# Relative bias loaded in two parts behind a branch chunk, attention outputs behind dense tiles, squares gathered on VectorE

## Chip, cores and metric

The kernel runs on one core of a Trainium2 chip. The metric is the device time in microseconds of one execution. One number is the median of several runs; the profile is of one further execution, with its own time.

## What is computed

Two layers of a decoder trunk on 512 tokens of width 1024, all in float32. Cut to what matters here:

```
x += 1/2 * gate1 * postnorm(SwiGLU(mod(prenorm(x))))     # feed-forward 1, width 2816
x +=       gate2 * postnorm(HybridMixer(mod(prenorm(x))))
x += 1/2 * gate3 * postnorm(SwiGLU(mod(prenorm(x))))     # feed-forward 2
# HybridMixer: one projection into GLA / differential attention / S5 / branch gates,
# each branch projected (w_branch[0..2]), merged by sigmoid gates, then w_out
logits = q @ k.T + bias[t5_bucket(dist)]                 # 8 maps, 4 heads of two maps
a = softmax(map 0) - lam * softmax(map 1);  o = a @ v;  o *= rsqrt(mean(o*o))
y *= rsqrt(mean(y*y, axis=-1) + 1e-6) * norm_post        # the post-norm of each sub-layer
```

## The kernel before

Activations lie transposed (channel on the partition, 512 tokens along the free axis). The weights come as chunks of 1 MB. SyncE loads each chunk into one of two places `raw[0]`, `raw[1]`; ScalarE copies it to a high part (`split`, L1278) and VectorE subtracts to get the low part (L1745). Each dense product is three matmuls, high by high, high by low and low by high (`matmul3`, L633 to L635); a tile of 128 outputs by 512 tokens with 8 input blocks is 24 matmuls, one with 4 input blocks is 12. A load waits until the split of the chunk two places earlier is done, a split waits until TensorE is done with that chunk. Every engine runs its own list in order, written out by hand; semaphores tie them.

**The mixer.** The list `MIXER` orders the chunks. Around the change they are `glu1, glu0, bs0, bs1, dq0, dq1, dk0 ... dv1, gg0, gg1, bg0, gg2, gg3, bg1, gd0 ...`, then `wo0..wo3` (the output projection). `ys` is the split of the S5 branch output, which `bs0` multiplies; the GLA decays (`gla_alpha` on TensorE, L1624 to L1636 on ScalarE, L2397 to L2412 on VectorE) run beside `dq0` and `dq1`. After the GLA heads (`o_ready` counts them) the GLA output `gr` is split into `yga_hi` (ScalarE, L1535) and `yga_lo` (VectorE, L2240), and `bg0` multiplies it. ScalarE and VectorE each split `bg0`: ScalarE before its `yga` splits, VectorE after them.

**The bias.** `bias_tab` (8 maps, 128 by 512 each, 2 MB) takes the place of `gq`, `gk`, `gv`, so SyncE waits for `o_ready` of all four GLA heads, then issues eight DMAs of 16 partitions (L613), and only then the load of `bg0`. VectorE waits for all eight before `diff_max` of step 0.

**The attention loop** has 16 steps i, head hd = i // 4, query block qb = i % 4. In step i TensorE does `diff_scores(i + 1)` (L1082), at the first step of a new head `diff_out` of the head before (L1098), one dense tile of `BESIDE_DIFF[i]`, at that same step `head_ms` (L1045, sums of squares of the head's output), and `diff_turn(i)` (transposes, L1091). VectorE does `diff_max(i + 1)` (bias and row maximum, L2285), at a new head `head_keep` (L2244, waits for `head_ms`), then `diff_mix(i)` (L2297 to L2300 and L1738), on which `diff_turn(i)` waits. ScalarE does the exponentials (L1555), `head_squares` at a new head (L1540, L1543), the sigmoids of gate tiles (L1461) and `diff_copy(i)` (L1565).

**A boundary** follows each of the six sub-layers (q = 0..5; 1 and 4 are the mixers', 5 the last). As each of the 8 output tiles ends, ScalarE copies it scaled to `y_sub` (L1321) and squares it to `sq_buf` (L1324); VectorE multiplies `y_sub` by `h` and adds up the products (L1793, L1798); TensorE adds the squares over channels with one block of 8 small matmuls per tile (`y_square_sums`, L647: column 0 plain, column 1 weighted by `sum_w`), each issued one tile late. After the last tile `norms` issues the blocks of tiles 6 and 7, the cross sums (`cross_total`, `cross_last`, L654), and then the root (L1342), its spread over rows (L675) and the normalization follow, before the next sub-layer can start.

## Time and profile before

| | |
|---|---|
| median of 3 runs | 2732.19 us (2730.94 to 2732.38) |
| the profiled execution | 2733.83 us, its span 2731.9 us |
| TensorE busy with matmuls | 2654.0 us, 97% |
| VectorE busy | 1396.2 us, 51% |
| ScalarE busy | 963.1 us, 35% |
| DMA engines | 35.2% of 16, mean 112 GB/s |
| mean granted TensorE clock | 0.979 of full |

All stretches below are in microseconds from the start of the span. The start of one instruction to the start of the next on TensorE is what it costs there; the printed length also holds the pipeline and is longer.

### The profile page before, as it was taken

Reading aid. Unit: us, or ns where it says so; the run is one execution under the profiler, and the core shown is the slowest. Engines: PE = TensorE matmul, PEld = TensorE weight load, DVE = VectorE, ACT = ScalarE, POOL = GpSimd, SP = SyncE. Lnnn points to the kernel's source line nnn. Section 1 sums busy time; section 2 is a strip of 40 time slices with the busy share of each in tenths; the row PEclk is TensorE's granted clock in tenths of the full one; section 3 lists DMA queues with packets and bytes.
Section 4 is the critical chain, followed back from the end, with each engine's and each line's share of the span. In section 5 each row is a group of like instructions: output and inputs, shape, how many; then the busy total and the mean of one; then the engine's idle time right before and its main releaser. Section 6 shows DMA issues by size and latency. Waiting matters only on the chain.

```text
span 2731.9 us, 34428 instructions
## 1 busy us (share of the span) xinstructions
PE 2654.0 (97%) x12925; PEld 2210.4 (81%) x12925; DVE 1396.2 (51%) x2146; ACT 963.1 (35%) x1177; POOL 75.1 (3%) x64
## 2 busy tenths in 40 slices
PE   6999999999989999999999999999999899999998
PEld 5888888987866888888888888899878578888886
DVE  5777326755245558532277752386342545653322
ACT  3333224644245432222142221346332643322212
POOL 0000001200000000000000000031000000000000
PEclk7999999999999999999999999999999999999999
DMA  8675222222241236322247633222223212332321
GB/s 260 200 229 178 100 92 74 78 70 93 62 93 61 79 108 213 126 92 100 100 139 231 225 113 104 74 82 78 87 86 62 83 62 93 108 123 95 105 92 47
DMA packets 268426, 306.99 MB, mean 112 GB/s; under 512 B 17783, under 2 KB 245499, under 8 KB 268324
## 3 DMA queue, kind: packets, MB, share of 16 engines
q1 hardware_dynamic: 268172, 305.23, 35.2%
q8 instruction: 71, 1.16, 0.2%
q10 hardware_dynamic: 152, 0.35, 0.0%
q14 instruction: 31, 0.25, 0.0%
HBM read 303.44 MB, written 2.45 MB: 112 GB/s over the span
## 4 chain that ended last, share of the span: by engine, by line
PE 91%; DVE 3%; ACT 2%; DMA 2%; issue 1%; SPq 1%; ACTq 0%; DVEq 0%
PE bank L633 26%; PE bank L635 25%; PE bank L634 25%; DMA raw<-in_w_branch 1%; PE bank L898 1%; PE bank L647 1%; PE bank L899 1%; PE bank L900 1%; PE bank L765 1%; PE bank L1098 1%; PE bank L1215 1%; PE bank L1062 1%; PE bank L1082 1%; PE bank L964 1%; PE bank L980 1%
## 5 line engine op out<-in xcount | busy, mean ns | idle before, releaser
L1745 DVE TENSOR_TENSOR w_both_lo<-raw,w_both_hi 128x2048 fp32r<-128x2048 f32 x200 | 459.6, 2298 | 619.5 <-ACT w_both_hi L1278 618.8
L633 PE MATMUL bank<-u_hi,w_both_hi 128*128 128x512 f32 x1928 | 763.0, 396 | 5.3 <-DVE u_lo L1738 2.6
L635 PE MATMUL bank<-u_hi,w_both_lo 128*128 128x512 f32 x1928 | 753.1, 391 | 0.0
L634 PE MATMUL bank<-u_lo,w_both_hi 128*128 128x512 f32 x1928 | 752.3, 390 | 0.0
L1278 ACT ACTIVATE w_both_hi<-raw 128x2048 fp32r<-128x2048 f32 x200 | 380.4, 1902 | 731.4 <-PE bank L635 702.3
L633 PEld LDWEIGHTS bank<-u_hi,w_both_hi 128*128 128x128 f32 x1928 | 363.4, 188 | 89.0 <-issue 7.5
L635 PEld LDWEIGHTS bank<-u_hi,w_both_lo 128*128 128x128 f32 x1928 | 362.9, 188 | 77.7
L634 PEld LDWEIGHTS bank<-u_lo,w_both_hi 128*128 128x128 f32 x1928 | 363.5, 189 | 73.0
L633 PE MATMUL bank<-g_hi,w_both_hi 128*128 (+1 forms) x704 | 276.2, 392 | 0.0
L635 PE MATMUL bank<-g_hi,w_both_lo 128*128 (+1 forms) x704 | 274.0, 389 | 0.0
L634 PE MATMUL bank<-g_lo,w_both_hi 128*128 (+1 forms) x704 | 274.0, 389 | 0.0
L1738 DVE SCALAR_TENSOR_TENSOR ada_acc<-ada_w,cond,ada_acc 128x256 f32<-128x256 f32 x448 | 217.2, 485 | 16.0
L1376 ACT ACTIVATE g_hi<-silu_buf 128x512 f32 (+1 forms) x88 | 55.6, 632 | 317.5 <-DVE silu_buf L1871 317.4
L635 PEld LDWEIGHTS bank<-g_hi,w_both_lo 128*128 128x128 f32 x704 | 132.1, 188 | 27.7
L634 PEld LDWEIGHTS bank<-g_lo,w_both_hi 128*128 128x128 f32 x704 | 132.3, 188 | 26.7
L633 PEld LDWEIGHTS bank<-g_hi,w_both_hi 128*128 128x128 f32 x704 | 132.2, 188 | 26.5
L1871 DVE TENSOR_TENSOR silu_buf<-silu_buf,bank 128x512 f32<-128x512 f32 x88 | 60.2, 686 | 182.4 <-PE bank L635 182.4
L898 PE MATMUL bank<-w_both_hi,u_hi 128*128 128x256 f32 x256 | 75.9, 297 | 0.0
L900 PE MATMUL bank<-w_both_lo,u_hi 128*128 128x256 f32 x256 | 72.5, 283 | 0.0
L899 PE MATMUL bank<-w_both_hi,u_lo 128*128 128x256 f32 x256 | 72.4, 283 | 0.0
L1875 DVE TENSOR_TENSOR g_lo<-silu_buf,g_hi 128x512 f32 (+1 forms) x88 | 60.5, 689 | 17.8 <-ACT g_hi L1376 17.7
L1321 ACT ACTIVATE y_sub<-bank,post_gain 128x512 f32<-128x512 f32 x48 | 32.9, 686 | 91.2 <-PE bank L635 90.9
(392 smaller groups left out, 3175.3 us busy)
## 6 DMA issues: line engine op xcount, KB each, us to landing
raw<-in_ffn_w_up SPq DMA_DIRECT2D x88, 1024.0 KB, 5.1
ada_w<-in_w_ada SPq DMA_DIRECT2D x64, 1024.0 KB, 5.0
raw<-in_w_in SPq DMA_DIRECT2D x52, 1024.0 KB, 5.2
raw<-in_ffn_w_down SPq DMA_DIRECT2D x44, 1024.0 KB, 4.8
raw<-in_w_branch SPq DMA_DIRECT2D x12, 1024.0 KB, 5.0
first_ada_w<-in_w_ada SPq DMA_DIRECT2D x8, 1024.0 KB, 12.2
raw<-in_w_out SPq DMA_DIRECT2D x8, 1024.0 KB, 4.9
raw<-in_s_w_glu SPq DMA_DIRECT2D x4, 1024.0 KB, 5.0
```

The source lines that it names most:

```text
L633: pe.matmul(dst, hi, rhi, start=first, stop=False)
L634: pe.matmul(dst, hi, rlo, start=False, stop=False)
L635: return pe.matmul(dst, lo, rhi, start=False, stop=last)
L898: pe.matmul(dst, u_hi[:, kt, tok], wh[:, kt, :], start=kt == 0, stop=False)
L899: pe.matmul(dst, u_lo[:, kt, tok], wh[:, kt, :], start=False, stop=False)
L900: m = pe.matmul(dst, u_hi[:, kt, tok], wl[:, kt, :], start=False, stop=kt == KT - 1)
L1278: act.activation(w_hi[s][:, 0:elems], raw[s][:, 0:elems], ACT.Copy).then_inc(hi_split[s].sem, 1)
L1376: act.activation(flat(g_hi[:, cols(j * 2 + mt), :]), silu_buf[:, mt, :], ACT.Copy).then_inc(g_hi_ready.sem, 1)
L1738: return v.scalar_tensor_tensor(out=o, in0=a, scalar=s, in1=b, op0=op0, op1=op1)
L1745: v.tensor_tensor(w_lo[s][:, :], raw[s][:, :], w_hi[s][:, :].bitcast(F32), SUB).then_inc(lo_split[s].sem, 1)
L1871: v.tensor_tensor(silu_buf[:, mt, :], silu_buf[:, mt, :], bank[2 + mt][:, :], MUL).then_inc(prod_done.sem, 1)
L1875: v.tensor_tensor(flat(g_lo[:, cols(j * 2 + mt), :]), silu_buf[:, mt, :], flat(g_hi[:, cols(j * 2 + mt), :]).bitcast(F32), SUB).then_inc(g ...
```

## The change

It changes the order of the attention's loads and steps, and where squares are added.

- SyncE loads `bg0` before it waits for `o_ready`; then maps 0 and 1 of the bias in eight DMAs, then `gg2`, then maps 2 to 7 in eight DMAs. VectorE waits for the second part in step 3, before `diff_max(4)`.
- In a head's first step `diff_out` stands behind the dense tile; `head_ms` moves to the second step, behind its tile; ScalarE's `head_squares` stands behind the sigmoid of the gate tile, VectorE's `head_keep` behind `diff_mix` of the second step.
- At the mixer boundaries (q = 1, 4) VectorE adds the squares of tiles 0 to 6, plain and weighted. TensorE sums both with 8 matmul calls, and does `cross_total`, inside the last tile (`gathered_sums`). The last tile's cross product is taken from the bank and a product `h` by gain made before; its copy to `y_sub` comes after that.
- At the last boundary VectorE adds the plain squares of tiles 0 to 6, TensorE sums them once after the last tile, and ScalarE squares the last tile before copying it. `sq_buf` is used with four slots at these boundaries; slots 4 and 5 hold the sums.
- Both engines split `dq1` ahead of the GLA exponentials and scans; VectorE splits `ys` tile by tile between the `glu0` tiles.

```
                 for name, _, _ in MIXER[17:26]:
                     load_chunk(L, name)
+                def load_bias(begin, end, loaded):
+                    for a in range(P // BIAS_COPIES):
+                        lines = bass.AP(tensor=bias_copies.tensor, offset=P - 1 - BIAS_COPIES * a + begin * BIAS_COPIES * LINE,
+                                        ap=[[LINE - 1, BIAS_COPIES], [BIAS_COPIES * LINE, end - begin], [1, SEQ]])
+                        sp.dma_start(bias_tab[BIAS_COPIES * a:BIAS_COPIES * (a + 1), begin:end, :], lines).then_inc(loaded.sem, 16)
                 sp.wait_ge(o_ready.sem, o_ready.of(L, GLA_HEADS))
...
+                load_bias(0, 2, first_bias_loaded)
+                load_chunk(L, MIXER[26][0])
+                load_bias(2, N_MAPS, bias_loaded)
+                for name, _, _ in MIXER[27:]:
...
+            def gathered_sums(L, ui):
+                begin_sums(3 * TB)
+                pe.wait_ge(sq_gathered.sem, sq_gathered.of(L, 2 * KT - 3))
+                for b in range(TB):
+                    pe.matmul(sums[:, 2 * b:2 * b + 1], plain_sq[:, b * P:(b + 1) * P], sum_w[:, ui, 0, 0:1], start=False, stop=False)
+                for b in range(TB):
+                    x = pe.matmul(sums[:, 2 * b + 1:2 * b + 2], scaled_sq[:, b * P:(b + 1) * P], ones[:, 0:1], start=False, stop=False)
+                x.then_inc(sq_summed.sem, KT - 1)
+                cross_total(3 * L + ui, 0)
...
             def norms(L, ui, order):
-                y_square_sums(q, ui, KT - 2, order[KT - 2])
-                if q < BOUNDARIES - 1:
+                if q == BOUNDARIES - 1:
+                    pe.wait_ge(last_gathered, KT - 2)
+                    begin_sums(3 * TB)
+                    for b in range(TB):
+                        x = pe.matmul(sums[:, 2 * b:2 * b + 1], plain_sq[:, b * P:(b + 1) * P], sum_w[:, ui, 0, 0:1], start=False, stop=False)
+                    x.then_inc(sq_summed.sem, KT - 1)
+                elif ui != 1:
+                    y_square_sums(q, ui, KT - 2, order[KT - 2])
+                if q < BOUNDARIES - 1 and ui != 1:
                     cross_total(q, order[0])
                 y_square_sums(q, ui, KT - 1, order[KT - 1])
...
+                    if within and kt == n - 2:
+                        within(L, 1)
...
                     if i + 1 < DIFF_HEADS * TB:
                         diff_scores(L, *divmod(i + 1, TB))
-                    if hd and qb == 0:
-                        diff_out(L, hd - 1)
                     for name, k in BESIDE_DIFF[i]:
                         chunk_tile(L, name, k, (yga_hi, yga_lo, 4, YGA) if name[0] == "b" else None)
                     if hd and qb == 0:
+                        diff_out(L, hd - 1)
+                    if hd and qb == 1:
                         head_ms(L, 4 + hd - 1, 7)
                     diff_turn(L, hd, qb)
...
                 for m in WIDE_ORDER:
-                    chunk_tile(L, f"wo{m // 2}", m % 2, (mg_hi, mg_lo, 8, MG))
-                    if 1 <= m < KT - 1:
-                        y_square_sums(3 * L + 1, 1, m - 1, m - 1)
+                    chunk_tile(L, f"wo{m // 2}", m % 2, (mg_hi, mg_lo, 8, MG), gathered_sums if m == KT - 1 else None)
...
             def y_tile(q, i, m, bk):
...
+                from_bank = q % 3 == 1 and i == KT - 1
+                last = q == BOUNDARIES - 1
+                if last and i >= 4:
+                    act.wait_ge(last_gathered, max(i - 4, 1))
+                if last and i == KT - 1:
+                    act.activation(sq_buf[:, sq_slot(q, i), :], bank[bk][:, :], ACT.Square).then_inc(sq_ready.sem, 1)
+                if not from_bank:
+                    act.activation(y_sub[:, m, :], bank[bk][:, :], ACT.Identity, scale=post_gain[:, g:g + 1]).then_inc(y_copied.sem, 1)
+                if q % 3 == 1 and i >= 4:
+                    act.wait_ge(sq_gathered.sem, sq_gathered.of(q // 3, 2 * max(i - 4, 1) + 1))
...
+                if from_bank:
+                    act.wait_ge(cross_ready.sem, cross_ready.of(q, KT))
+                    act.activation(y_sub[:, m, :], bank[bk][:, :], ACT.Identity, scale=post_gain[:, g:g + 1]).then_inc(y_copied.sem, 1)
...
+            def gather_squares(q, i):
+                L, sq, weight = q // 3, sq_buf[:, sq_slot(q, i), :], sum_w[:, 1, i, 1:2]
+                v.wait_ge(sq_ready.sem, sq_ready.of(q, i + 1))
+                if i == 0:
+                    v.tensor_scalar(scaled_sq, sq, weight, None, MUL, ALU.bypass).then_inc(sq_gathered.sem, 1)
+                else:
+                    v.wait_ge(sq_gathered.sem, sq_gathered.of(L, 2 * i - 1))
+                    stt(scaled_sq, sq, weight, scaled_sq, MUL, ADD).then_inc(sq_gathered.sem, 1)
+                    v.tensor_tensor(plain_sq, sq_buf[:, sq_slot(q, 0), :] if i == 1 else plain_sq, sq, ADD).then_inc(sq_gathered.sem, 1)
...
+                    if q % 3 == 1 and i == KT - 1:
+                        v.wait_ge(gain_ready.sem, gain_ready.of(q // 3, 1))
+                        v.wait_ge(sq_ready.sem, sq_ready.of(q, KT))
+                        v.tensor_tensor(cross[:, m, :], cross[:, m, :], bank[TILES["wo3", 1].bank][:, :], MUL).then_inc(cross_ready.sem, 1)
...
+                    if q % 3 == 1 and i < KT - 1:
+                        gather_squares(q, i)
...
             def last_boundary(q):
+                for i in range(1, KT - 1):
+                    v.wait_ge(sq_ready.sem, sq_ready.of(q, i + 1))
...
+                    v.tensor_tensor(plain_sq, sq_buf[:, 0, :] if i == 1 else plain_sq, sq_buf[:, sq_slot(q, i), :], ADD)\
+                     .then_inc(last_gathered, 1)
```

## Rows read from the trace of the kernel before

**Rows 1.** The page, busy time of the engines.
```profile
PE 2654.0 (97%) x12925; PEld 2210.4 (81%) x12925; DVE 1396.2 (51%) x2146; ACT 963.1 (35%) x1177; POOL 75.1 (3%) x64
```
**Rows 2.** Who waited for whom, TensorE: us in total, times, longest us.
```profile
PE bank L1082 <- DVE smax L2289: 18.1, 2, 9.8
PE bank L1091 <- DVE prob L1738: 10.3, 9, 1.6
...
PE bank L633 <- DVE ys_lo L2240: 3.3, 2, 1.7
...
PE bank L633 <- DVE w_both_lo L1745: 2.4, 2, 1.2
```
**Rows 3.** The chain that ended last, 755 to 800: start, us, what.
```profile
766.26 19.42 DMA raw<-in_w_branch
```
**Rows 4.** Timeline, SyncE's queue, layer 0: start, us, what.
```profile
762.46 3.70 SPq L613 DMA_DIRECT2D bias_tab<-bias_copies_dram  x8
```
**Rows 5.** Windows: length, busy of PE, PEld, DVE, ACT, POOL, clock, DMA share, GB/s.
```profile
770.00:774.00 4.00, 4.00 (x24) 3.32 (x24) 2.79 (x4) 0.60 (x1) 0.00 (x0) 1.00 1.09 123
824.00:828.00 4.00, 4.00 (x12) 2.61 (x10) 3.69 (x10) 2.59 (x6) 0.00 (x0) 0.57 0.28 60
2149.00:2155.00 6.00, 6.00 (x31) 5.05 (x29) 0.00 (x0) 3.06 (x8) 0.00 (x0) 1.00 0.00 0
```
**Rows 6.** Timeline around the first scores, layer 0, then layer 1.
```profile
776.69 0.69 DVE L2259 TENSOR_TENSOR gr<-gr,o_head 128x512 f32<-128x512 f32 x1
...
787.52 2.17 ACT L1535 ACTIVATE yga_hi<-gr 128x512 fp32r<-128x512 f32 x4
...
793.54 1.23 PE L1082 MATMUL bank<-dk,dq 64*128 64x256 f32 x4 [9.77 <-DVE smax L2289]
...
804.01 0.44 PE L1091 MATMUL bank<-ident,prob 128*128 128x128 f32 x2 [1.34 <-DVE prob L1738]
...
2111.49 0.69 DVE L2259 TENSOR_TENSOR gr<-gr,o_head 128x512 f32<-128x512 f32 x1
...
2120.83 2.17 ACT L1535 ACTIVATE yga_hi<-gr 128x512 fp32r<-128x512 f32 x4
```
**Rows 7.** Timeline of TensorE at changes of head, both layers.
```profile
812.84 0.70 PE L1082 MATMUL bank<-dk,dq 64*128 64x256 f32 x4
...
831.72 0.38 PE L1091 MATMUL bank<-ident,prob 128*128 128x128 f32 x2
...
845.66 0.70 PE L1082 MATMUL bank<-dk,dq 64*128 64x256 f32 x4
847.79 2.42 PE L1098 MATMUL bank<-a_t,dv 128*128 128x512 f32 x8 [1.43 <-ACT a_t L1565]
...
862.13 0.38 PE L1091 MATMUL bank<-ident,prob 128*128 128x128 f32 x2
...
2146.14 0.70 PE L1082 MATMUL bank<-dk,dq 64*128 64x256 f32 x4
...
2163.46 0.38 PE L1091 MATMUL bank<-ident,prob 128*128 128x128 f32 x2
...
2177.40 0.70 PE L1082 MATMUL bank<-dk,dq 64*128 64x256 f32 x4
...
2192.59 0.44 PE L1091 MATMUL bank<-ident,prob 128*128 128x128 f32 x2 [1.57 <-DVE prob L1738]
```
**Rows 8.** Timeline of the end of the mixer boundary, layer 0.
```profile
1001.75 0.95 PE L647 MATMUL bank<-sum_w,sq_buf 128*128 128x2 f32 x8
...
1003.46 1.03 PE L647 MATMUL bank<-sum_w,sq_buf 128*128 128x2 f32 x8
...
1005.49 0.26 ACT L1342 ACTIVATE roots<-bank,cst 128x4 f32<-128x4 f32 x1 [2.36 <-PE bank L654]
```
**Rows 9.** Timeline of the last boundary.
```profile
2710.07 0.95 PE L647 MATMUL bank<-sum_w,sq_buf 128*128 128x2 f32 x8
...
2712.59 0.26 ACT L1342 ACTIVATE roots<-bank,cst 128x4 f32<-128x4 f32 x1 [1.14 <-PE bank L647]
```

More of the change, by code:

```diff
@@ L823, in bank_free, with chunk_tile @@
                     pe.wait_ge(emptied[last.engine].sem, emptied[last.engine].of(L, last.emptied))
-            def chunk_tile(L, name, k, src=None, part=None):
+            def chunk_tile(L, name, k, src=None, within=None, part=None):
                 ch = chunk_of(L, name)
@@ L1621, in _ @@
                 split_chunk(L, "dq0")
+                split_chunk(L, "dq1")
                 for t in range(2):
@@ L1681, in _ @@
                             empty(L, name, k)
+                    if hd and qb == 0:
+                        head_squares(L, 4 + hd - 1, 7)
                     diff_copy(L, i)
@@ L1818, in boundary @@
                 v.wait_ge(y_rstd_ready, q + 1)
+                v.wait_ge(y_copied.sem, y_copied.of(q, KT))
                 scaled = scale_y(q, 0)
@@ L2382, in _ @@
                         .then_inc(emptied["vec"].sem, 1)
+                    if k:
+                        split_tile(L, YS, k - 1, ys_lo, ys_hi, z_gate[:, k - 1, :])
                 v.wait_ge(emptied["vec"].sem, emptied["vec"].of(L, 4))
-                for k in range(4):
-                    split_tile(L, YS, k, ys_lo, ys_hi, z_gate[:, k, :])
+                split_tile(L, YS, 3, ys_lo, ys_hi, z_gate[:, 3, :])
                 split_chunk(L, "bs1")
@@ L2398, in _ @@
                      .then_inc(alpha_read.sem, 1)
+                split_chunk(L, "dq1")
                 for t in range(2):
```

46 lines of the change are left out of this document (26 added, 20 removed).

## The prediction

> **What bounds the kernel now.** I read the page first: TensorE is busy 97% of the span [rows 1], so time can only come from work taken off TensorE, from its waits, or from stretches at a low clock. Second, the view of who waited for whom, for TensorE alone. Its waits sum to some 70 us; some 22 of these lie in the start and a few at the boundaries, and the change touches four groups [rows 2]: two waits of 18.1 us in all for VectorE's row maxima (`diff_max`), 10.3 us in nine waits for the mixed probabilities, 3.3 us for `ys_lo`, 2.4 us for the low part of `dq1`. Third, the chain that ended last: it runs through TensorE, except where it stands for 19.42 us on the load of `bg0` [rows 3]. Fourth, the timelines of those places, to see what each wait hangs on, and the windows for the clock.
>
> **The bias.** SyncE issues eight DMAs at 762.46 and needs 3.70 us [rows 4]; only then comes `bg0`, at 766.26. While the 2 MB run, the queue moves 123 GB/s [rows 5], so they take 2 MB / 123 = 17 us and `bg0` lands behind them. ScalarE has the split of `bg0` ahead of its four `yga_hi`, and so starts these at 787.52, though `gr` was complete at 776.69 + 0.69 = 777.38 [rows 6]. Everything to the next transposes hangs on that start: `yga_lo`, the low split of `bg0`, `diff_max(0)`, then the exponentials, the split of `gg2` and `diff_mix(1)`; the chain takes 804.01 - 787.52 = 16.5 us.
> With the change `bg0` is issued before 762 (its place is free once `gg0` is split) and is landed long before TensorE leaves `gg0`; ScalarE splits it while it now stands idle, and `yga_hi` starts at 777.4. The chain is 10.1 us earlier. TensorE can take that: its dense work before the wait ends at 793.54 - 9.77 = 783.8, and `diff_max(0)` is then ready at 783.4, so the scores come 0.4 us behind the chain, which has slack there. Layer 1 by the same two rows: 2120.83 - 2112.18 = 8.6. Sum 18.7.
> The wait of 1.34 us at 804.01 is not removed but grows, since the dense tiles between run at full clock again and end earlier; this gain of clock is already inside the 10.1. Lower end: only part of the waits, 16 (18.1 less 2 for a first part that comes late); upper end: the chain shortens as well, 21.
> What is late next? The first part is 0.5 MB, by 123 GB/s 4.3 us after an issue of 3.7: landed near 771, wanted at 782.7. `gg2` and the second part (1.5 MB, 12 us) go out by 771 and are landed by about 787; `gg2` is wanted by ScalarE at 786, the second part only in step 3, near 799. So the eight added DMAs cost SyncE 3.7 us in which it has nothing due: `gg3` waits for the split of `bg0` at 782.7 anyway and is split in step 4. If that cover were gone, each us of delay would cost one.
> The Trainium skill (DMA: Bandwidth & Descriptors, Rules for kernel authors) speaks against this part: many small transfers are to be put together, and under 64 KB one pays mostly overhead; the pieces of the first part are exactly 64 KB. Its table (section Bandwidth) has 138 GB/s at 64 KB against 341 at 1 MB, so by it the first part would take 3.8 us, an estimate, and the sum stays. No row here has a piece of 64 KB, and the rule only adds to the chance of the last rival.
>
> **The changes of head**, three per layer. Before, at a head's first step, `diff_out` can wait for the copy (1.43 us [rows 7]), and `head_keep` on VectorE holds up `diff_mix` and so the transposes by 1.1 us each; six such are among the 10.3 us [rows 2]. Behind the wait the clock falls: 0.57 at 824 to 828, against 1.00 beside the tiles of the same kind in layer 1 [rows 5], that is partly at 1.2 GHz. Two steps from scores to transposes take 831.72 - 812.84 = 18.88 in layer 0 and 2163.46 - 2146.14 = 17.32 in layer 1, the same work [rows 7]; without the 1.11 wait 16.2.
> After, `diff_out` stands behind 2.8 or 5.5 us of dense work, when its copy and `diff_mix` are done, and `head_ms` a step later, where ScalarE's squares (1.2 us) had a whole tile's time. `head_keep` waits behind `diff_mix(5)`; behind it on VectorE only the next step's branch tile and `diff_max(7)` queue, whose scores are issued after `head_ms` anyway.
> First change: 18.88 - 16.2 = 2.7 in layer 0, 1.1 in layer 1. Second: layer 1 has 2192.59 - 2177.40 = 15.19 with waits of 1.43, 1.11 and 1.57, which leaves 11.1, so 4.1; layer 0 has 862.13 - 845.66 = 16.47, so 5.4. The third of both layers has the wait and the low clock of the first in layer 0, 2.7 each. Sum 2.7 + 1.1 + 5.4 + 4.1 + 5.4 = 18.7. Ends: 11 if the low clock stays, 20 if more of it goes.
>
> **The mixer boundaries** (two). A block of square sums costs TensorE 1001.75 to 1003.46 for it and `cross_total`, 0.86 each, and 0.04 at the restart of the dense tile [rows 8]: 0.9. Six blocks leave the stream: 5.4. From the last tile's end, 1001.75, to the root, 1005.49, it is 3.74. After, it is: ScalarE's square 0.2 + 0.6, the last block 0.86, `cross_last` 0.9 (the cross product, 0.7, beside the block), 0.15 for the root: 2.7, so 1.0 saved. Put into the last tile: 16 small matmuls like two blocks, 1.7, and `cross_total` with the restart, 0.75 to 1.0. Net 5.4 + 1.0 - 2.5 = 4.0 each, 8.0 for both.
> VectorE gets for each tile two instructions of 0.7, the length of one of 128 by 512 [rows 6], in a tile's time of 5.5 us with 1.4 of old work and now and then a split of 2.3. The tight place is tile 6: from its end copy 0.9, cross 0.7, two gathers 1.4, gain 0.5, sum 0.7, so the totals are there at 4.3 of the 4.9 us after which TensorE wants them (the gathers at 3.1, the cross total 1.8 us after 4.9), and two half splits of 1.2 end at 6.7, before the last square at about 8.9. ScalarE's `y_sub` copy (0.7) runs beside `cross_last`. Ends: 5 if the short stop after the last tile lowers the clock by 1.5 us each, 8.8.
>
> **The last boundary.** Six blocks leave, 5.4. Tiles now follow in 1.4 us; ScalarE needs 1.3 for copy and square, so it just keeps up. From last tile to root: 2.52 now [rows 9]; after: gathered at 0.8, 8 matmuls and the start 1.05, last block 0.85, 0.1: 2.8. Net 5.2; ends 4.4 (ScalarE paces) and 6.
>
> **Two orders.** `dq1` is split 2.2 us earlier in time in which both engines stand; the wait of 2.4 goes (ends 2.0, 2.4). `ys` tile by tile: only the last low part, 0.7 behind its high part, is left, wanted as fourth block: of 3.3 I count 3.2 (ends 2.6, 3.3). The exponentials and the split of `bs1` behind them become earlier, not later.
>
> **The sum.** 18.7 + 18.7 + 8.0 + 5.2 + 2.4 + 3.2 = 56.2. Against the profiled execution's own 2733.83 that is 2677.6. Its span lies 1.9 below its time and the work around it doesn't change. It stood 1.6 above the median of the runs, so 2676. The ends sum to 41 and 61.5: 2691 to 2671.
>
> **Rivals.**
> *The low clock stays at the changes of head* (17 in 100). For it: the small transposes and scores remain. Against: in layer 1 the same work with the same wait kept 1.00 [rows 5]. Four places of 1.5 to 2: 7.5 less, 2683.5.
> *VectorE is late at tile 6 and the boundary gains go* (10 in 100). The slack there is 0.6 us; from one more split or wait on it TensorE stops inside the last tile. All 8.0 lost: 2684.
> *The bias parts do little* (6 in 100): a second wait stands behind the first, so TensorE waits for `gg2` or the second part instead. Half of 18.7 lost: 2685.
> *Several of these together* (5 in 100): 2694.
> *Slower* (2 in 100): the eight pieces of the first part land late, each with a fixed delay one after another. It costs where it lands later than 783, and outweighs the other gains (37.5, or 19 per layer) and the present wait from landing near 812, 50 us after the issue; at 60 us it gives 2752. The eight pieces of 256 KB now need 17 us, which speaks against it.
>
> **Chances.** My forecast 60 in 100. Faster by over 0.2% 97, within it 1, slower 2; 0.2% is about what a measurement of this kernel can tell from no change. The range takes the ends of the terms and most of the first three rivals: 2668 to 2692.
>
> **What would show it.** Right: `bg0` lands before 762, the wait before the second scores is under 1 us in both layers; no wait of 1.1 us at L1091 after L1045, clock near 1.0 there; 8 L647 matmuls at the mixer boundary instead of 64, with 16 before `cross_total` in the last tile and no stop there; tiles of 1.4 us at the last boundary. Wrong: a wait of VectorE on `bias_tab`, a stop inside `wo3`'s last tile, a granted clock near 0.6 in the step after `diff_out`.

## The result, and the profile after

| | before | after |
|---|---|---|
| median | 2731.64 us (2730.94 to 2732.38, 4 runs) | 2682.01 us (2681.22 to 2682.32, 4 runs) |
| profiled execution, span | 2733.83, 2731.9 us | 2681.22, 2679.5 us |
| mean granted clock | 0.979 | 0.982 |

The ratio is 0.9818, with a 95% interval of 0.9803 to 0.9833: the changed kernel is 1.8% faster. The medians are 49.6 us apart, the profiled executions 52.6; the terms of the prediction summed to 56.2, and its 2676 is 6.0 below the median. The line numbers have moved: the dense matmuls are L647 to L649, the scores L1116 (before L1082), the transposes L1125 (L1091), `diff_out` L1132 (L1098), `head_ms` L1079 (L1045), the blocks of square sums L661 (L647), the cross sums L668 (L654), the low splits L1790 (L1745).

The page, busy time of the engines:

```profile
PE 2633.3 (98%) x12797; PEld 2195.4 (82%) x12797; DVE 1416.5 (53%) x2180; ACT 963.5 (36%) x1177; POOL 75.1 (3%) x64
```

TensorE lost 20.7 us of busy time against [rows 1], VectorE gained 20.3. The other 31.7 of the 52.4 us between the two spans are waits. Who waited for whom, TensorE, after (us in total, times, longest):

```profile
PE bank L1125 <- DVE prob L1783: 5.3, 2, 2.7
...
PE bank L661 <- ACT sq_buf L1366: 1.4, 2, 0.7
...
PE bank L653 <- DVE sq_buf L1912: 0.6, 1, 0.6
```

Of the four groups of [rows 2] three are gone: no wait for the maxima ahead of the second scores, none for `ys_lo`, none for the low part of `dq1`. Of the nine waits for the mixed probabilities two are left, one in each layer, and they are longer than any before, 2.65 us. Two new ones of 0.7 stand at the mixer boundaries. At the last boundary one of 0.6 has taken the place of one of 0.5, which was for the last tile's square.

**The loads.** SyncE's queue in layer 0, and the profile's list of DMA issues from 755 to 800 (queue, count, size of each, median us from issue to landing; its `raw<-in_w_branch` is the later `bg1`, and the list from 746 to 752 has the same row for `bg0`):

```profile
748.40 0.37 SPq L492 DMA_DIRECT2D raw<-in_w_branch  x1
...
760.30 3.61 SPq L621 DMA_DIRECT2D bias_tab<-bias_copies_dram  x8
764.02 0.39 SPq L492 DMA_DIRECT2D raw<-in_w_in  x1
```
```profile
bias_tab<-bias_copies_dram SPq DMA_DIRECT2D x8, 192.0 KB, 10.6
raw<-in_w_branch SPq DMA_DIRECT2D x1, 1024.0 KB, 4.9
bias_tab<-bias_copies_dram SPq DMA_DIRECT2D x8, 64.0 KB, 2.2
```

`bg0` is issued at 748.40, 14 us before the bias DMAs of [rows 4] were issued, and lands 4.9 us later. The pieces of the first part need 2.2 us each. That part is complete near 766 and wanted at 780.5. The 19.42 us of [rows 3] are gone from the chain, which reads here, from the start of the splits to the transposes of step 1 (start, us, what):

```profile
775.25 0.64 ACT yga_hi L1580
...
778.41 2.20 DVE w_both_lo L1790
...
788.10 0.69 DVE sig L2344
...
791.22 0.49 DVE prob L1783
...
791.76 0.44 PE bank L1125 x2
```

`yga_hi` starts 12.3 us earlier than in [rows 6]; 2.2 of these were gained ahead of it. TensorE has no dense work left at 789.11 and stands until 791.76. This is the stop that is left; layer 1 has the same, 2.66. Ahead of the two branch products (`sig`, `merged`) VectorE's list has the low part of `gg2`:

```profile
785.89 2.29 DVE L1790 TENSOR_TENSOR w_both_lo<-raw,w_both_hi 128x2048 fp32r<-128x2048 f32 x1 [1.59 <-ACT w_both_hi L1310]
```

**The clock**, in windows (length, busy time of PE, PEld, DVE, ACT and POOL, clock, DMA share, GB/s):

```profile
793.00:797.00 4.00, 4.00 (x12) 2.83 (x11) 2.69 (x10) 1.52 (x4) 0.00 (x0) 0.59 0.00 0
800.00:804.00 4.00, 4.00 (x21) 2.82 (x20) 3.63 (x12) 2.67 (x6) 0.00 (x0) 1.00 0.02 4
...
976.00:982.00 6.00, 5.35 (x24) 4.95 (x25) 1.67 (x7) 1.84 (x4) 0.00 (x0) 0.60 0.36 126
2284.00:2290.00 6.00, 5.31 (x22) 4.72 (x22) 1.67 (x7) 1.56 (x4) 0.00 (x0) 0.54 0.40 140
```

The first row is behind the stop of step 1 in layer 0: 12 matmul records in 4 us instead of 21, a granted clock between its two levels of 1.2 and 2.4 GHz. The last two rows hold the ends of the two mixer boundaries. Between 800 and the boundary no such stretch is left, where [rows 5] had 0.57 at 824.

**The changes of head**, TensorE, layer 0 and then layer 1:

```profile
801.95 0.70 PE L1116 MATMUL bank<-dk,dq 64*128 64x256 f32 x4
...
808.17 2.32 PE L1132 MATMUL bank<-a_t,dv 128*128 128x512 f32 x8
...
816.95 0.95 PE L1079 MATMUL bank<-inv_d,o_sq 128*128 128x1 f32 x8
817.76 0.42 PE L1125 MATMUL bank<-ident,prob 128*128 128x128 f32 x2
...
831.73 0.70 PE L1116 MATMUL bank<-dk,dq 64*128 64x256 f32 x4
...
842.12 0.41 PE L1125 MATMUL bank<-ident,prob 128*128 128x128 f32 x2
...
2110.16 0.70 PE L1116 MATMUL bank<-dk,dq 64*128 64x256 f32 x4
...
2125.96 0.42 PE L1125 MATMUL bank<-ident,prob 128*128 128x128 f32 x2
...
2139.93 0.70 PE L1116 MATMUL bank<-dk,dq 64*128 64x256 f32 x4
...
2150.33 0.41 PE L1125 MATMUL bank<-ident,prob 128*128 128x128 f32 x2
```

No row waits. The same two steps take 15.81 in layer 0 and 15.80 in layer 1 (2125.96 - 2110.16) where [rows 7] had 18.88 and 17.32, and at the second change 10.39 and 10.40 where it had 16.47 and 15.19: 3.1, 1.5, 6.1 and 4.8 us. Layer 0 and layer 1 now agree. Before, at the first change, they had the same wait and differed by 1.6, with a clock of 0.57 in layer 0 and 1.00 in layer 1 [rows 5]; that much was the clock.

**A mixer boundary**, layer 0, the last tile and what follows:

```profile
972.21 0.28 PE L653 MATMUL bank<-no_w,ident 128*128 128x12 f32 x2
...
973.24 1.03 PE L705 MATMUL bank<-ones,sq_buf 128*128 128x1 f32 x8
...
975.58 0.39 PE L649 MATMUL bank<-mg_hi,w_both_lo 128*128 128x512 f32 x1
976.00 0.60 ACT L1366 ACTIVATE sq_buf<-bank 128x512 f32<-128x512 f32 x1 [6.23 <-PE bank L649]
976.65 1.41 PE L661 MATMUL bank<-sum_w,sq_buf 128*128 128x2 f32 x8 [0.69 <-ACT sq_buf L1366]
...
977.93 1.84 PE L668 MATMUL bank<-cross_w,cross 128*128 128x1 f32 x8
...
979.81 0.26 ACT L1387 ACTIVATE roots<-bank,cst 128x4 f32<-128x4 f32 x1 [1.70 <-PE bank L668]
```

The gathered sums stand inside the last tile, without a wait: VectorE is in time. The tile ends at 975.58 + 0.23 = 975.81, its last block starts 0.84 later and takes 1.28, the cross sums 1.7 and more, where [rows 8] show 0.86 for such a block. The root starts 4.0 behind the tile's end, 4.45 in layer 1. In [rows 8] it was 3.74, with every block still at full speed.

**The last boundary:**

```profile
2657.52 0.39 PE L653 MATMUL bank<-no_w,ident 128*128 128x12 f32 x2 [0.64 <-DVE sq_buf L1912]
2657.76 1.03 PE L717 MATMUL bank<-sum_w,sq_buf 128*128 128x1 f32 x8
2658.65 1.03 PE L661 MATMUL bank<-sum_w,sq_buf 128*128 128x2 f32 x8
2659.72 0.26 ACT L1387 ACTIVATE roots<-bank,cst 128x4 f32<-128x4 f32 x1 [1.63 <-PE bank L661]
```

From the last tile's end, 2656.72, to the root it is 3.0; in [rows 9] it was 2.52. The tiles ahead follow in 1.36 us.

**Where the time came from.** Each term is read as the change of the distance between the same instructions of the two traces, ahead of the edit and behind it; the last column is the part alone, by medians, from the experiments below.

| term | priced | in the two traces | alone (from the 95% interval of its ratio) |
|---|---|---|---|
| bias behind `bg0`, in two parts | 18.7 | 8.7 + 8.6 = 17.3 | 14.4 (9.6 to 16.7) |
| changes of head | 18.7 | 12.1 + 9.3 = 21.4 | 18.2 (15.3 to 22.4) |
| mixer boundaries | 8.0 | 2.7 + 2.2 = 4.9 | 4.1 (-0.3 to 4.4) |
| last boundary | 5.2 | 5.4 | 6.4 (4.1 to 9.0) |
| the two orders | 5.6 | 2.87 + 2.86 = 5.7 | 4.8 (1.6 to 6.6) |
| sum | 56.2 | 54.7 | 47.9 |

Of the 54.7 the traces give back 0.7 in the start of the kernel, 1.2 between the root of the first mixer boundary and `ys` of layer 1, where two feed-forward boundaries stand, and 0.5 behind the last root. The change touches none of the first two stretches. 54.7 - 0.7 - 1.2 - 0.5 = 52.3, and the spans are 52.4 apart.

### The profile page after: what moved, and what is told of

The parts are those of the page before. It is cut to its first block, busy times and chain, and to the rows that moved or that the text cites. A ratio compares the mean times of both kernels' runs of the same rounds, so it can differ in the third digit from the quotient of the medians.

```text
span 2679.5 us, 34250 instructions
## 1 busy us (share of the span) xinstructions
PE 2633.3 (98%) x12797; PEld 2195.4 (82%) x12797; DVE 1416.5 (53%) x2180; ACT 963.5 (36%) x1177; POOL 75.1 (3%) x64
## 4 chain that ended last, share of the span: by engine, by line
PE 94%; DVE 3%; ACT 1%; SPq 1%; issue 1%; DMA 0%; ACTq 0%; DVEq 0%
PE bank L647 27%; PE bank L649 26%; PE bank L648 26%; PE bank L932 1%; PE bank L934 1%; PE bank L933 1%; PE bank L797 1%; PE bank L661 1%; PE bank L1116 1%; PE bank L1132 1%; PE bank L1247 1%; PE bank L1096 1%; PE bank L998 1%; PE bank L1014 1%; PE bank L1079 0%
## 5 line engine op out<-in xcount | busy, mean ns | idle before, releaser
L1790 DVE TENSOR_TENSOR w_both_lo<-raw,w_both_hi 128x2048 fp32r<-128x2048 f32 x200 | 459.7, 2298 | 620.6 <-ACT w_both_hi L1310 619.9
L647 PE MATMUL bank<-u_hi,w_both_hi 128*128 128x512 f32 x1928 | 761.4, 395 | 2.9 <-DVE u_lo L1783 2.6
L649 PE MATMUL bank<-u_hi,w_both_lo 128*128 128x512 f32 x1928 | 751.9, 390 | 0.0
L647 PEld LDWEIGHTS bank<-u_hi,w_both_hi 128*128 128x128 f32 x1928 | 362.5, 188 | 86.7 <-issue 8.4
L649 PEld LDWEIGHTS bank<-u_hi,w_both_lo 128*128 128x128 f32 x1928 | 362.2, 188 | 77.0
L647 PE MATMUL bank<-g_hi,w_both_hi 128*128 (+1 forms) x704 | 275.6, 392 | 0.0
L649 PE MATMUL bank<-g_hi,w_both_lo 128*128 (+1 forms) x704 | 274.0, 389 | 0.0
L649 PEld LDWEIGHTS bank<-g_hi,w_both_lo 128*128 128x128 f32 x704 | 132.1, 188 | 27.7
L647 PEld LDWEIGHTS bank<-g_hi,w_both_hi 128*128 128x128 f32 x704 | 132.2, 188 | 26.7
L1344 ACT ACTIVATE u_hi<-mod_buf,ada 128x512 fp32r<-128x512 f32 x48 | 34.7, 725 | 84.3 <-DVE mod_buf L1783 84.3
## 6 DMA issues: line engine op xcount, KB each, us to landing
first_ada_w<-in_w_ada SPq DMA_DIRECT2D x8, 1024.0 KB, 12.3
```

The costliest lines, as they stand in the source:

```text
L647: pe.matmul(dst, hi, rhi, start=first, stop=False)
L649: return pe.matmul(dst, lo, rhi, start=False, stop=last)
L1790: v.tensor_tensor(w_lo[s][:, :], raw[s][:, :], w_hi[s][:, :].bitcast(F32), SUB).then_inc(lo_split[s].sem, 1)
```

## The experiments

Each ratio is to the kernel before in the same set of runs. Its median was 2731.97 beside the bias, the heads and the two boundaries alone, 2731.4 beside the orders, the bias in one part, the three spare matmuls and the later `gg2`, 2731.7 beside the next three and 2730.96 beside the last. The changed kernel itself was not run again beside the later ones: where a kernel is set against its 2682.01, or against another set's median, the sets' own medians of the kernel before differ by up to 1.0.

**The bias and `bg0` alone**, on the kernel before.

```
-                for name, _, _ in MIXER[17:25]:
+                for name, _, _ in MIXER[17:26]:
...
+                load_bias(0, 2, first_bias_loaded)
+                load_chunk(L, MIXER[26][0])
+                load_bias(2, N_MAPS, bias_loaded)
```

> Only the order of the loads: bg0 ahead of the wait for the heads, the bias in two parts around gg2. Theory A (the chain from the yga split to the second transposes moves by 10.1 and 8.6 us, and what the chain gains TensorE partly gives back where it now stops for 2.7 us and falls to the low clock, 1.3 us in one layer): 17 to 18.7 us faster than before, near 2714. Rival B (the bias part brought all it was priced at, the shortfall lies elsewhere): 18.7, 2713. Rival C (the bias part brought half): 2722. In the trace A wants a stop of over 2 us before the second transposes of both layers and a low clock behind at least one.

Measured: 2717.61 (2716.3 to 2720.59), ratio 0.9952 [0.9939, 0.9965], 14.4 less. That is under the 17 of theory A, which is also outside the interval (9.6 to 16.7 us). The profiled executions are 17.5 apart, since 2716.37 lies 1.2 below its median and 2733.83 lies 1.9 above the median of before. In its trace the wait for the maxima is gone in both layers and the stop of step 1 is as in the whole:

```profile
794.96 0.44 PE L1097 MATMUL bank<-ident,prob 128*128 128x128 f32 x2 [2.65 <-DVE prob L1744]
```

So this stop comes with the bias part alone.

**The changes of head alone.**

```
-                    if hd and qb == 0:
-                        diff_out(L, hd - 1)
...
                     if hd and qb == 0:
+                        diff_out(L, hd - 1)
+                    if hd and qb == 1:
                         head_ms(L, 4 + hd - 1, 7)
...
-                    if hd and qb == 0:
+                    diff_mix(L, i)
+                    if hd and qb == 1:
                         head_keep(L, 4 + hd - 1, 7)
-                    diff_mix(L, i)
```

ScalarE's `head_squares` moves behind the gate tiles, as in the whole change.

> Only the attention outputs and head sums behind dense tiles, on all three engines, bias as before. Theory A (the changes of head brought more than priced, 21 instead of 18.7, because the low clock goes at all of them): 21 us faster, 2711. Rival B (18.7 as priced): 2713. Rival C (the low clock stays): 11 us, 2721. The waits of 1.1 us before the transposes must be gone in all.

Measured: 2713.78 (2710.64 to 2715.44), ratio 0.9931 [0.9918, 0.9944], 18.2 less. Against the trace of before the six changes gave 12.1 in layer 0 and 9.4 in layer 1, as in the whole.

**The mixer boundaries alone** (`gathered_sums`, the gathering on VectorE and the cross product from the bank, with q = 1 and 4 only).

```
-                    if 1 <= m < KT - 1:
-                        y_square_sums(3 * L + 1, 1, m - 1, m - 1)
...
+                    if q % 3 == 1 and i < KT - 1:
+                        gather_squares(q, i)
```

> Only the two mixer boundaries: squares gathered on VectorE, summed in the last tile, last cross product from the bank. Theory A (TensorE stops for 0.7 us after the last tile with only small matmuls around it, the clock falls and the two small blocks cost 1.3 and 1.7 instead of 0.9 each): 4.9 us faster for both, 2726.7. Rival B (priced right, 8.0): 2723.6. Rival C (VectorE is late and TensorE stops inside the last tile): 2731 or more. In the trace: 4.0 us from the last tile's end to the root by A, 2.7 by B.

Measured: 2727.92 (2724.73 to 2733.99, 12 runs), ratio 0.9992 [0.9984, 1.0001], 4.1 less. The interval holds 1, so this part alone is not told from no change by time; that it acts is read from the traces. From the last tile's end to the root its trace has 4.69 and 4.70 us, where [rows 8] had 3.74 and theory A 4.0: here the clock fell 1.4 and 1.7 us before the last tile's end, so before the stop.

**The last boundary alone.**

```
+                if q == BOUNDARIES - 1:
+                    pe.wait_ge(last_gathered, KT - 2)
+                    begin_sums(3 * TB)
+                    for b in range(TB):
+                        x = pe.matmul(sums[:, 2 * b:2 * b + 1], plain_sq[:, b * P:(b + 1) * P], sum_w[:, ui, 0, 0:1], start=False, stop=False)
```

> Only the last boundary: plain squares of tiles 0 to 6 added on VectorE and summed once. Both theories: 5.0 to 5.4 us faster, 2726.4; A adds that the spread of the root afterwards runs at the low clock and costs 0.5 of it. A rival in which ScalarE sets the pace of the tiles would give 4.4 or less and tiles over 1.4 us apart.

Measured: 2725.59 (2722.57 to 2728.28, 11 runs), ratio 0.9976 [0.9967, 0.9985], 6.4 less; across the boundary its trace gains 5.4 on that of before.

**The two orders alone** (`dq1` split ahead of the exponentials and scans, `ys` tile by tile).

```
+                    if k:
+                        split_tile(L, YS, k - 1, ys_lo, ys_hi, z_gate[:, k - 1, :])
...
+                split_chunk(L, "dq1")
```

> On the kernel before, only the two orders: dq1 split ahead of the GLA exponentials, ys split tile by tile. As priced 5.6 us faster, near 2726; the waits of 1.2 us before dq1 and of 1.7 us before bs0 must be gone in both layers. A rival: the later GLA exponentials hold up the key transposes and 1 to 2 us come back there, 2728.

Measured: 2726.57 (2722.99 to 2730.57, 11 runs), ratio 0.9985 [0.9976, 0.9994], 4.8 less.

The five parts alone sum to 47.9 us, the whole gave 49.6. Each of the five is known to some 2.5 or 3.5 us, so the two agree, and this says no more than that the parts do not cancel or double each other by more than a few us.

**The changed kernel with the bias in one part**, behind `bg0` and ahead of `gg2`.

```
-                load_bias(0, 2, first_bias_loaded)
-                load_chunk(L, MIXER[26][0])
-                load_bias(2, N_MAPS, bias_loaded)
-                for name, _, _ in MIXER[27:]:
+                load_bias(0, N_MAPS, bias_loaded)
+                for name, _, _ in MIXER[26:]:
```

> On the changed kernel, the bias in one part again (eight DMAs, all maps), but behind bg0; gg2 behind it. Theory A (the gain comes from bg0 going ahead of the 2 MB, not from the two parts: 2 MB at 123 GB/s from 760 land at 778, VectorE wants them at 780): the same within 1 us, 2682. Rival (the split in two matters): VectorE waits for the bias and ScalarE for gg2, 2 to 8 us slower, 2684 to 2690. In the trace the wait of VectorE before the first row maximum and of ScalarE before the split of gg2 tell it.

Measured: 2681.67 (2680.62 to 2682.26), ratio 0.9817 [0.9804, 0.9831], against 2682.01 of the changed kernel. What gains is `bg0` ahead of the bias; the two parts buy nothing, and the sixteen smaller DMAs cost nothing.

**The changed kernel with three spare matmuls in the stop of each mixer boundary.**

```
+                if ui == 1:
+                    pe.wait_ge(lo_split[ch % 2].sem, slot_value(lo_split[ch % 2], ch))
+                    fill(ch, 3)
                 y_square_sums(q, ui, KT - 1, order[KT - 1])
```

> On the changed kernel, three matmuls of 512 columns that nobody reads (0.7 us) in the stop after the last tile of the mixer boundaries. It computes the same. Theory A (the stop lets the clock fall and that costs 1.2 us in the two small blocks): 2 us faster for both boundaries, 2680, the blocks back at 0.9 each, the root 2.8 us after the last tile instead of 4.0. Rival (small matmuls alone hold the clock down, or the blocks are slow for another reason, such as ScalarE and VectorE reading beside them): no change, 2682, blocks still at 1.3 and 1.7.

Measured: 2679.38 (2678.4 to 2679.81), ratio 0.9809 [0.9796, 0.9823]; no run of it is as slow as the fastest of the changed kernel. Windows over the ends of its two boundaries:

```profile
974.00:980.00 6.00, 5.93 (x37) 4.60 (x36) 3.60 (x12) 1.83 (x4) 0.00 (x0) 1.00 0.37 129
2282.00:2288.00 6.00, 6.00 (x25) 5.55 (x25) 1.68 (x7) 1.25 (x3) 0.00 (x0) 0.50 0.25 88
```

In layer 0 the clock stays at 1.00, the last block takes 0.9, and the root follows here, 2.83 behind the tile's end:

```profile
975.55 1.03 PE L668 MATMUL bank<-cross_w,cross 128*128 128x1 f32 x8
...
976.62 0.26 ACT L1390 ACTIVATE roots<-bank,cst 128x4 f32<-128x4 f32 x1 [0.53 <-PE bank L668]
```

In layer 1, with the same spare matmuls and no stop, the clock falls to 0.50 all the same and the root comes 4.46 behind. So the stop is not needed for the low clock there, and filling it does not always keep the clock up.

**The changed kernel with the split of `gg2` in step 2 instead of 0.**

```
-BESIDE_SPLIT = {0: "gg2", 4: "gg3", 6: "bg1", 8: "gd0", 12: "gd1", 14: "gd2"}
+BESIDE_SPLIT = {2: "gg2", 4: "gg3", 6: "bg1", 8: "gd0", 12: "gd1", 14: "gd2"}
```

> On the changed kernel, both engines split gg2 in step 2 instead of step 0. Theory A (the stop of 2.65 us before the second transposes hangs on the high and low split of gg2, 1.9 and 2.3 us, that stand in ScalarE's and VectorE's lists ahead of the second step's work): the stop shrinks to under 0.5 us in both layers and the low clock behind it goes: 4 to 6 us faster, 2677. Rival (another wait takes its place in step 2 or 3, for the split there delays the exponentials and the mix): 0 to 2 us faster, 2681, with a stop before the transposes of step 2 or 3.

Measured: 2680.56 (2677.59 to 2683.79), ratio 0.9814 [0.98, 0.9827]: its runs lie on both sides of the changed kernel's. The stop leaves step 1 and comes back in step 3, with the low clock behind it, in both layers (1.68 and 1.67):

```profile
799.24 0.66 PE L1125 MATMUL bank<-ident,prob 128*128 128x128 f32 x4 [1.68 <-DVE prob L1783]
```
```profile
800.00:804.00 4.00, 4.00 (x13) 2.73 (x14) 3.26 (x11) 3.37 (x6) 0.00 (x0) 0.58 0.11 39
```

Up to the transposes of step 2 this trace gains 4.2 us on the changed kernel's, and behind the stop and the low clock only 0.7 are left. In layer 1, where the changed kernel has no low clock behind its stop, it loses 0.6. In both of the places tried the split of 2.3 us makes one step's transposes late.

This trace also shows where the clock falls at its mixer boundaries. In layer 0 the last tile ends at 976.14, and the cross sums within the tile already take 1.44 us instead of the 1.03 of the changed kernel:

```profile
973.61 1.44 PE L668 MATMUL bank<-cross_w,cross 128*128 128x1 f32 x8
```
```profile
974.00:976.00 2.00, 2.00 (x9) 1.72 (x8) 0.00 (x0) 0.00 (x0) 0.00 (x0) 0.52 0.78 245
```

The clock falls 2.1 us ahead of the tile's end, 1.9 in layer 1, before there is any stop and before the 16 small matmuls behind the tile; what runs there are the small matmuls within the tile.

**The changed kernel with VectorE's branch tile last in each step.**

```
-                    for name, k in BESIDE_DIFF[i - 1] if i else ():
-                        if name[0] == "b":
-                            branch_tile(L, name, k, 4 * int(name[-1]) + k)
...
                     if hd and qb == 1:
                         head_keep(L, 4 + hd - 1, 7)
+                    for name, k in BESIDE_DIFF[i - 1] if i else ():
+                        if name[0] == "b":
+                            branch_tile(L, name, k, 4 * int(name[-1]) + k)
```

> The changed kernel, with one order on VectorE turned round: in each step the old branch tile is multiplied and added behind diff_max of the next step and diff_mix of this one, no more ahead of them. Theory A (the stop of 2.65 us that is left ahead of the transposes of step 1 hangs on VectorE's order: after the low split of gg2 at 788.18 come the branch tile, 1.4, diff_max(2), 1.1, and only then diff_mix(1)): the transposes start 1.4 earlier in each layer, at 790.4 instead of 791.76 in layer 0, the stop is 1.2 to 1.3, and the time is 2 x 1.4 less, 2679.2, or about 2678 if the low clock behind the stop goes too. Rival B (the branch tile then frees its bank late, or the next step's maxima come as late as now): the stop moves into step 2 or 3 with its whole length, as it did when the split was moved to step 2, and the time stays within 1 us of 2682.

Measured: 2675.86 (2674.75 to 2676.99), ratio 0.9795 [0.9782, 0.9809], 6.1 less than the changed kernel. VectorE and the transposes of step 1:

```profile
788.21 0.55 DVE L2359 CUSTOM_DVE_ANT_0 prob<-bank,bias_tab 128x384 f32<-128x384 f32 x1
...
790.01 0.48 DVE L1783 SCALAR_TENSOR_TENSOR prob<-prob,smax 128x256 f32<-128x256 f32 x1
790.41 0.68 DVE L2344 TENSOR_TENSOR sig<-sig,bank 128x512 f32<-128x512 f32 x1
790.54 0.44 PE L1125 MATMUL bank<-ident,prob 128*128 128x128 f32 x2 [1.34 <-DVE prob L1783]
```

The maxima follow the split at once, the branch tile comes behind `diff_mix`, and the stop is 1.3 instead of 2.65 in both layers. In layer 0 the low clock behind it is gone too: 2.7 us there, 1.3 in layer 1, 4.0 of the 6.1 by the traces. The edit does not tell whether the clock stays up because the stop is shorter: in layer 1 of the changed kernel it stayed up behind the whole 2.65. The rest is not pinned to a place: the traces differ by 0.7 in layer 1 ahead of the mixer, and otherwise by stretches of low clock that come and go.

**The changed kernel with spare matmuls in all stops**: the three at the mixer boundaries, eight in step 1, two at the last boundary.

```
+                if q == BOUNDARIES - 1:
+                    fill(ch - 1, 2)
...
+                    if i == 1:
+                        fill(chunk_of(L, "bg0"), 8)
                     diff_turn(L, hd, qb)
```

> The changed kernel with the three spare matmuls in the stop of both mixer boundaries (2679.38), and two more sets: eight of them (1.8 us) in the stop of 2.65 us ahead of the transposes of step 1, two (0.46 us) in the stop of 0.64 us at the last boundary. Theory A (each stop leaves the clock low behind it in some executions, and what fills it keeps the clock up): in no place behind these stops is the granted clock under 1.0, the row that follows the last stop takes 0.65 instead of 1.11, and the time is 0.5 to 1.5 below that of the three alone, 2678 to 2679. Rival B (at these two places the stop itself is all that is lost, the clock behind it is lowered by the small matmuls): 2679.4, within 0.5. Rival C (the fillers run late and push the work behind them): up to 1 slower, 2680.4.

Measured: 2679.54 (2678.38 to 2680.38), ratio 0.9809 [0.9796, 0.9823]: the same as with the three alone. In the trace the signs of theory A are there: of the stop of 2.65 only 0.83 stays empty, the clock behind it is 1.00 in both layers, and the row behind the last root takes 0.65. Still the median gains nothing, as rival B had it. At the last boundary the root comes 0.47 later, 3.47 behind the tile's end, which takes back what the row behind it gains. The stop there stands ahead of the gathered sums and I had put the two spare matmuls behind these, so they fill nothing and cost their 2 x 0.23; what filling that stop would do was not tried, and the eight in step 1 were not tried without these two.

**On the kernel before, `head_keep` alone moved**, on VectorE's list; TensorE and ScalarE keep theirs.

```
                     if i + 1 < DIFF_HEADS * TB:
                         diff_max(L, i + 1)
-                    if hd and qb == 0:
+                    diff_mix(L, i)
+                    if hd and qb == 1:
                         head_keep(L, 4 + hd - 1, 7)
-                    diff_mix(L, i)
```

> The kernel before with one thing moved, on VectorE alone: head_keep goes from ahead of diff_max in a head's first step to behind diff_mix in its second. TensorE's and ScalarE's order stay. Theory A (the six waits of 1.1 us at L1091 and the low clock behind them come from head_keep alone, which waits for TensorE and holds up diff_mix): the six waits go, 6.6, and of the low clock behind them about half, so 2722 to 2725 against 2731.5; the waits of diff_out for its copy (1.4) stay, and these are the rest of the 18.2 that the whole move gave. Rival B (TensorE's own wait for ScalarE's squares at head_ms is the one that counts, VectorE only waits beside it): the wait moves from L1091 to L1045, and the time stays within 2 us of 2731.5.

Measured: 2716.38 (2714.57 to 2717.37), ratio 0.9942 [0.9928, 0.9956], 15.3 less, of the 18.2 of the whole move. Its first change of head, and `diff_out` at the second:

```profile
811.74 0.70 PE L1082 MATMUL bank<-dk,dq 64*128 64x256 f32 x4
...
820.28 0.95 PE L1045 MATMUL bank<-inv_d,o_sq 128*128 128x1 f32 x8
...
827.78 0.38 PE L1091 MATMUL bank<-ident,prob 128*128 128x128 f32 x2
...
843.86 2.42 PE L1098 MATMUL bank<-a_t,dv 128*128 128x512 f32 x8 [1.43 <-ACT a_t L1565]
```

827.78 - 811.74 = 16.04 against 18.88 in [rows 7], 2.8 of the 3.1. The wait of `diff_out` stays, with 1.43. I had put only half of the low clock on `head_keep`, 6.6 to 9.5 in all; it was nearly all of it (no low clock is left at a change of head in this trace either), and the rival that TensorE's own wait for the squares counts is out.

**The two edits that gained, together**: the branch tile last, and three spare matmuls at the mixer boundaries.

> The changed kernel with the two edits that gained: the branch tile last on VectorE (2675.86, that is 6.1 less than the changed kernel) and three spare matmuls in the stop of both mixer boundaries (2.6 less). Theory A (the two act at different places and add): 2682.0 - 6.1 - 2.6 = 2673.3, within 1. Rival B (both gain by the same thing, less low clock somewhere in the mixer, which can be had once): 2675 to 2676, as the first alone.

Measured: 2673.02 (2672.9 to 2676.86), ratio 0.9794 [0.9781, 0.9808]. It is 9.0 below the changed kernel, where the two alone sum to 8.8. But its five executions fall into two groups, three at 2672.9 to 2673.0 (mean clock 0.986) and two at 2676.8 to 2676.9 (0.983), and the second group is no faster than the kernel with the branch tile last alone. The profiled execution is of the second, 2676.83.

**What the spare matmuls do** can't be read from that trace. The distance from the last tile's end to the first matmul of the next sub-layer, layer 0 and 1, from the timelines:

| kernel | layer 0 | layer 1 |
|---|---|---|
| before | 9.60 | 9.48 |
| before, `head_keep` alone moved | 8.55 | 10.87 |
| mixer boundaries alone | 10.94 | 10.75 |
| changed | 10.25 | 10.32 |
| bias in one part | 10.25 | 10.25 |
| `gg2` in step 2 | 10.59 | 10.70 |
| branch tile last | 10.33 | 10.08 |
| three spare matmuls | 7.73 | 10.33 |
| spare ones in all stops | 8.66 | 11.40 |
| branch tile last and three spare | 11.43 | 11.40 |

The old order of the boundary too has a low clock in all of its traces but one, layer 0 of the kernel with `head_keep` moved:

```profile
990.00:1000.00 10.00, 9.52 (x61) 7.90 (x61) 5.64 (x15) 2.46 (x5) 0.00 (x0) 1.00 0.34 111
```

At full clock from end to end it is thus 8.55 in the old order and 7.73 in the new with three spare matmuls, 0.8 less; the 9.60 of before holds a low stretch behind the root. Of the fourteen mixer boundaries of the changed kernel and its six variants the clock held wholly in one and partly in one, both with spare matmuls. In three others with spare matmuls the way is 1.1 longer than in the changed kernel. The medians are 2.5 to 2.8 lower with them in three comparisons of three, one of them between groups that overlap, as said, and none between kernels run side by side. That they gain is measured so far; that they gain by the clock at these two places is seen in one boundary of one profile.

## Why the prediction was right, and where it was off

**Faster, and by these means: right.** All five terms are there, each at its place, and none of the rivals came. That the sum came within 1.5 us of the traces is in part luck: the heads were priced 2.7 too low and the mixer boundaries 3.1 too high. The low clock does not stay at the changes of head: in eight of the nine profiles of kernels that hold this move, or the move of `head_keep` alone, no stretch of dense matmuls is slowed there, and in the ninth, with `gg2` in step 2, it is the stop of step 3 that runs into the first change; while the profile of before has three such between 824 and 886 and one at 2213, of 1.6 to 2.6 us each (by how much longer than 0.39 us its matmuls of 512 columns are). VectorE is not late at tile 6. No second wait takes the place of the one for `bg0`, beyond the stop in step 1 that the prediction named. The first part of the bias does not land late.

**The bias**: 10.1 and 8.6 were priced; measured from the last `gr` of each layer, the transposes of step 1 come 10.1 and 8.6 earlier, to the tenth. What I wrote of the wait of 1.34, that it "is not removed but grows", is right too: it is 2.65. But I gave it no price, and behind it the clock falls in layer 0, 1.3 us. By medians the part alone is less still, 14.4, and 18.7 is outside its interval. With the branch tile last on VectorE half of this stop goes. What it hangs on is VectorE's order, 2.29 for the low part of `gg2` and then the branch tile, not a load; a gap of 1.3 us stays, and what would remove it was not found.

**The small pieces.** Eight DMAs of 64 KB landed 2.2 us after their issue, where the eight of 256 KB before needed 10.4 by the same list. From 760 to 764 they moved 98 GB/s at a DMA share of 0.39, where the pieces of before moved 123 at 1.09 [rows 5]. By the rule that I weighed, from the Trainium skill (DMA: Bandwidth & Descriptors, Rules for kernel authors), a transfer under 64 KB is mostly overhead. These pieces are exactly at its bound, and this trace shows nothing of such an overhead; by the times, 2682.01 against 2681.67 in one part, none reaches the end of this kernel.

**The changes of head**: priced 18.7, 21.4 in the traces, 18.2 alone by medians. By the terms: 3.1 and 6.1 instead of 2.7 and 5.4 in layer 0, 1.5 and 4.8 instead of 1.1 and 4.1 in layer 1, and 3.0 and 3.1 at the third changes instead of 2.7 each. Each is 0.3 to 0.7 under what came: I took 11.1 as the second change without waits, and it is 10.4. The share of VectorE's `head_keep` is shown by moving it alone: 15.3 us, where the whole move gave 18.2 in another set of runs. The prediction had the wait of `head_keep` and the clock behind it at full weight, and that was right.

**The mixer boundaries are the step that failed in size**: "Net 5.4 + 1.0 - 2.5 = 4.0 each, 8.0 for both"; the terms as printed make 3.9. They gave 4.9, which is my lower end of 5, "if the short stop after the last tile lowers the clock". Put into the last tile is 2.8 instead of 2.5 (972.21 to 975.03). From the last tile's end to the root I counted 2.7 and it took 4.0 and 4.45, since the two blocks ran mostly at the low clock (0.60 and 0.54 over their windows). With the clock at 1.00, in layer 0 of the kernel with spare matmuls, it took 2.83: the working of the 2.7 was right, its clock was not. The cause that I named for this end, the short stop, is not what brings the clock down in the traces that can tell. In layer 1 of the kernel with spare matmuls it fell with no stop at all. With `gg2` in step 2, and with the mixer boundaries alone, it fell in both layers 1.4 to 2.1 us before the last tile's end, at the end of the 24 small matmuls that the change puts within that tile. So the likely step that I had left out is that these 24 lower the clock for what follows; I had priced them by their length alone. It is not proved: no run has the gathered sums elsewhere or fewer of them, in some traces the clock falls only behind the tile, and in one it holds with the 24 in place.

**The last boundary** gave 5.4 for 5.2 (5.1 by its own numbers, 5.4 + 2.52 - 2.8) and lost 0.5 behind the root, in its spread over rows (1.11 us for 0.65 before, at the low clock). **The orders** gave 5.7 for 5.6.

**From 56.2 to the 6.0 us of the miss.** The spans are 52.4 apart, 3.8 less than the sum: 3.1 for the mixer, 1.4 for the bias with the clock behind step 1, 0.7 in the start, 1.7 behind the boundaries, less 2.7 for the heads and 0.4 elsewhere. With what lies around the span it is 52.6 and 3.6. Then I took 1.6 off for the profiled execution of before standing above its median. It does, by 2.2. But its low stretches lie for the most part where the change works, at the changes of head, and I had already counted them there as gained. If they are why it stands above its median, the 1.6 were taken twice; the heads alone, 18.2 by medians and 21.4 by the traces, fit that. So do the mean clocks: the profiled execution has 0.979, and of the 23 executions of before beside the first experiments the nine under 2731 us have 0.980 to 0.982, the fourteen over it 0.978 to 0.981. At which places the clock was low in them is not seen. The last 0.8 is that the profiled execution of after is faster than its median. 3.6 + 1.6 + 0.8 = 6.0.

## What to carry to other kernels

When a queue waits behind a bulk load for a small one that others need, put the small one first; splitting the bulk load is a second thought, and here it bought nothing. On an engine that others wait for, put what releases them first and its own bookkeeping last: moving `head_keep` behind `diff_mix` gave 15.3 us and moving the branch tile behind it 6.1, with not one instruction less. Small matmuls put into a dense stretch can cost more than their length: in two kernels here the clock was at its lower level from the last of them until past the root, in both layers. And when a profiled execution is slower than its median because of low clock, do not price its low stretches as gains and then subtract the difference once more.

## What the runs showed of the hardware that was not expected

- Behind waits of about 1 us at the changes of head the clock was low at some and not at others, in one execution and from one to the next; a stop of 2.65 us in step 1 had the low clock behind it in layer 0 of the changed kernel (0.59) and not in layer 1. It cost 1.3 to 2.6 us each time. The executions of the kernel before, 23 in one set, spread over 6.2 us (2727.58 to 2733.75).
- At the end of a mixer boundary the clock fell to 0.50 without any stop, and in two kernels to about 0.5 before the last tile had ended (0.52 from 974 to 976 with `gg2` in step 2, 0.50 from 993 to 994 with the mixer boundaries alone), at the end of 24 matmuls of 1 column. In the kernel before it stayed at 1.00 through most of the 32 small matmuls behind the last tile of layer 0 (1001.75 to 1005.00) and fell at the root.
- Spare matmuls of 0.23 us each, put where TensorE stands, took 2.6 us off the median at the mixer boundaries, and nothing where eight more filled most of the stop in step 1, with the clock at 1.00 behind it, and two more came too late at the last boundary.
